# A tenth place in two pieces for expert weights, and another order of gathers and scatters in the loop over experts

## The chip, the cores and the metric

One NeuronCore of a Trainium2 chip. The metric is the device time of one execution in microseconds, lower is better. Engines are named as in the profile: PE is TensorE, DVE VectorE, ACT ScalarE, POOL GpSimd, SP SyncE, whose queue issues nearly all DMAs.

## What is computed

Two transformer blocks on one sequence of 256 tokens of width 1024, all in 32-bit floats. The change lies in the mixture of experts that ends the first block: 32 experts, each token goes to its best ones, gates are a softmax over their logits.

```python
logits = (xt @ router_w + router_b).astype(jnp.float32)
top_vals, top_idx = lax.top_k(logits, TOP_K)
gates = jax.nn.softmax(top_vals, axis=-1)
...
    hcat = xblk @ w_up[e] + b_up[e]
    x_glu = jnp.minimum(hcat[:, 0::2], SWIGLU_LIMIT)
    x_lin = jnp.clip(hcat[:, 1::2], -SWIGLU_LIMIT, SWIGLU_LIMIT)
    act = x_glu * jax.nn.sigmoid(SWIGLU_ALPHA * x_glu) * (x_lin + 1.0)
    return act @ w_down[e] + b_down[e]
...
contrib = y_slots[dest] * gate_sorted[:, None]
out = jax.ops.segment_sum(contrib, tok_sorted, num_segments=N)
```

The second block multiplies two of its results by gate rows that come from a conditioning vector (`x + g1 * ...`, `x + g2 * ...`); the change moves the making of these rows too.

## The kernel before

The program is a row of blocks: `first_mix` (projections and two kinds of attention), `branches` (the rest of the first mix, layer norm, the router's logits and choice), `experts`, `second_mix` and `output`. Between blocks all engines meet.

**Weights of the experts.** An expert has 12 MB of weights: W_up in four chunks and W_down in two, 2048 KB each, rows of 16 KB for each of 128 partitions. Two experts are a pair of 12 chunks; 16 pairs make 192 chunks, numbered 0 to 191. In a pair come the four up chunks of the first expert, the four of the second, then two and two down chunks. Chunk i lies in place i mod 9 (`PLACES`): six places are pairs of slots of `ring`, place 5 (`EXTRA`) is the later two thirds of the buffer `x_xT_xn` (`k.wide`), places 7 and 8 are `more`. `load_expert` issues one DMA for a chunk. SP issues chunks 0 to 8 in `branches`, as their places come free there, and in `experts` `refill` issues chunk i when PE has counted chunk i - 9 as read (`used`, two counts for a chunk). The loop over pairs is unrolled three times (`LOOPED`), so that the places come round.

**A pair on PE** (`pair`). Only the tokens of an expert are worked on: a selection matrix (`keep_tri`) gathers them by matmul (`gather`, in two halves of four tiles, each copied to `xg` by ACT in `gathered`), and another (`selT`) scatters the results back. PE does: up chunks of the first expert (`up_weights`), waits for ACT's copy `hrow`, turns it (`units_turned`), scatters the results of the pair before into four banks (`scatter`), which DVE adds to `acc` (`added`, `collect`), up chunks of the second expert, waits for `hrow`, turns, down chunks of the first expert (`down_weights`), turns the gated selection, gathers both halves for the next pair, and does the down chunks of the second. In the last pair (`tail`) the second half-gather stands between its last two down chunks. Then come the closing products of `acc` with the identity (L1398) and the last scatter.

```python
up_weights(r, turn, at, n, 0)
units_turned(n, 0)
scatter()
up_weights(r, turn, at, n, 1)
units_turned(n, 1)
down_weights(r, turn, at, n, 0)
```

**Around it.** In `branches` DVE makes the gates (L1177 to L1180) and then the choice (L1184, `choose`) that the first gather waits for. ACT writes two diagonal matrices (L1045) from which PE, by products with ones (L965 there, L2154 in `output`), makes the gate rows `gB`; these lie in the first third of `x_xT_xn`. Short products of no use (`fill`) keep PE going in waits.

Of the kernel before, what the change touches and what calls it, by code (L numbers as in the profile page):

```python
# [14 lines left out]
F32 = mybir.dt.float32  # L15
# [3 lines left out]
ALU = mybir.AluOpType  # L19
# [37 lines left out]
UP_CHUNKS = 4  # L57

# [844 lines left out]
def branches(nc, k, a):  # L903
# [9 lines left out]
    gate_ready, gT_done = sem("gate_ready"), sem("gate_turned")  # L913
    gd, ang_ready = sem("gate_diag"), sem("angles")
    gb_done = k.gb_done
# [5 lines left out]
    with k.ctx_block("branches") as blk:  # L921
        @blk.sync
        def _(sp):
# [16 lines left out]
            for i in (MORE, MORE + 1):  # L940
                load_expert(k, sp, a, 0, i)

        @blk.tensor
        def _(pe):
# [18 lines left out]

            def gate_row(half):
                return nc.tensor.matmul(k.ps[:, half, :], k.ones[:, :], k.diag[0][:, half * 512:(half + 1) * 512],  # L965
                                        start=True, stop=True)
# [39 lines left out]
            pe.wait_ge(gd, 1)  # L1006
            logits(0, range(4)).then_inc(log_done, 1)
            gate_row(0)
# [4 lines left out]
            gate_row(1).then_inc(gb_done, 1)  # L1013
# [9 lines left out]
            pe.wait_ge(gate_ready, 1)  # L1023
            for t in range(TT):
                last = nc.tensor.transpose(k.ps[0:E, 6, t * P:(t + 1) * P], k.gate[:, t, :], k.ident[:, :])
            last.then_inc(gT_done, 1)
# [4 lines left out]
        def _(act):  # L1031
# [11 lines left out]
            for n, row in enumerate((GATE1, GATE2)):  # L1043
                for m in range(KD):
                    ins = nc.scalar.activation(k.diag[n][:, m * P:(m + 1) * P], k.ident[:, :], ACT.Copy,  # L1045
                                               scale=k.mod[:, row + m:row + m + 1])
            ins.then_inc(gd, 1)
# [14 lines left out]
            act.wait_ge(gb_done, 1)  # L1062
            act_copy(nc, k.gB[:, 0, :], k.flat[:, 0:1024])
            act.wait_ge(gT_done, 1)
            act.wait_ge(k.selT_zeroed, 1)
            act_copy(nc, k.selT[0:E, :], k.ps[0:E, 6, 0:T]).then_inc(k.selT_ready, 1)
# [35 lines left out]
        def _(dve):  # L1102
# [75 lines left out]
            link(nc.vector.tensor_reduce(k.small[:, 2:4], ex[:, :, :], AX.X, ALU.add))  # L1178
            link(nc.vector.reciprocal(k.small[:, 4:6], k.small[:, 2:4]))
            nc.vector.tensor_tensor(k.gate[:, :, :], ex[:, :, :], bc(k.small[:, 4:6], 2, E), ALU.mult).then_inc(gate_ready, 1)  # L1180

# [5 lines left out]
            nc.vector.tensor_scalar(k.place[:, :, E:E + 2], k.place[:, :, 0:2], float(-CAP), None, ALU.add)  # L1187

# [5 lines left out]

def expert_chunk(k, i):

    i %= PLACES
    if i == EXTRA:
# [4 lines left out]
    return k.ring[:, at:at + 2, :].rearrange("p s n -> p (s n)")  # L1203

# [6 lines left out]
def expert_arrived(k, pe, r, turn, i):  # L1211

    place = i % PLACES
    pe.wait_ge(k.expert_in[place], r * (16 * uses(place)) + turn * (16 * LOOPED * PAIR // PLACES) + 16 * (i // PLACES + 1))
    return expert_chunk(k, i)
# [13 lines left out]
def load_expert(k, sp, a, first, i):  # L1229
# [9 lines left out]
    sp.dma_start(expert_chunk(k, i), src).then_inc(k.expert_in[i % PLACES], 16)  # L1239


def experts(nc, k, a):
# [9 lines left out]
    hot_ready, g_done = k.hot_ready, k.g_done  # L1252
# [8 lines left out]
    scat = (up, rows)  # L1261
# [8 lines left out]
    with k.ctx_block("experts") as blk:  # L1270
# [37 lines left out]
        def _(pe):  # L1308
            def scatter(added=()):
                for t, out in enumerate(scat):  # L1310
# [5 lines left out]
            gather(nc, k, 5, range(4, KD)).then_inc(g_done, 1)  # L1316
            extra = extra_rounds(pe)

            def up_weights(r, turn, at, n, h):
                for q in range(KD):  # L1320
                    if h == 0 and q % 4 == 0:
# [3 lines left out]
                    w = chunk[:, (q % 2) * 2048:(q % 2 + 1) * 2048]  # L1325
# [16 lines left out]
            def down_weights(r, turn, at, n, h, halves=(0, 1)):  # L1342
# [3 lines left out]
                for j in (2 * v + w for v in halves for w in range(2)):  # L1346
                    if j % 2 == 0:
                        chunk = expert_arrived(k, pe, r, turn, at * PAIR + 2 * UP_CHUNKS + 2 * h + j // 2)
                    w = chunk[:, (j % 2) * 2048:(j % 2 + 1) * 2048]
# [1295 lines left out]
```

## Time and profile before

| | |
|---|---|
| median of three runs | 1529.42 us (1527.02 to 1530.88) |
| the profiled execution | 1528.25 us, span of its instructions 1526.5 us |
| busy, share of the span | PE 94%, DVE 38%, ACT 29%, POOL 3% |
| moved by DMA | 516.47 MB, mean 338 GB/s |
| mean granted TensorE clock | 0.998 |
| `experts`, by its first and last products on PE | about 264 to 1182 us |

All rows come from one profiled execution, with times from the start of its span. In a timeline a row is: start, duration, engine, line and operation, output and inputs, count, and in brackets how long the engine had stood idle and what ended that. Rows that follow each other on PE overlap a little, so lengths are better taken from one start to the next. Products of 32-bit floats are recorded as two instructions each (x16 for eight). In a table of stretches each row has the stretch, its length, the busy time of each engine, the granted clock (1.00 is 2.4 GHz), the busy share of the DMA engines and GB/s.

### The profile page before, as it was taken

Reading aid. Unit: us, or ns where it says so; the run is one execution under the profiler, and the core shown is the slowest. Engines: PE = TensorE matmul, PEld = TensorE weight load, DVE = VectorE, ACT = ScalarE, POOL = GpSimd, SP = SyncE. Lnnn points to the kernel's source line nnn. Section 1 sums busy time; section 2 is a strip of 40 time slices with the busy share of each in tenths; the row PEclk is TensorE's granted clock in tenths of the full one; section 3 lists DMA queues with packets and bytes.
Section 4 is the critical chain, followed back from the end, with each engine's and each line's share of the span. In section 5 each row is a group of like instructions: output and inputs, shape, how many; then the busy total and the mean of one; then the engine's idle time right before and its main releaser. Section 6 shows DMA issues by size and latency. Waiting matters only on the chain. (4 is left out here: it accounts for less than half of the span.)

```text
span 1526.5 us, 19835 instructions
## 1 busy us (share of the span) xinstructions
PE 1429.0 (94%) x8005; PEld 846.0 (55%) x8005; DVE 584.2 (38%) x978; ACT 449.3 (29%) x597; POOL 38.4 (3%) x80
## 2 busy tenths in 40 slices
PE   9999999999999999988988989889889999999998
PEld 9987898344334434323423433333333788888887
DVE  4985457211210211210210210210211685777765
ACT  5654543121111112111111111111111536553343
POOL 2000030000000000000000000000000022000000
PEclk9999999999999999999999999999999999999999
DMA  8597999899999999999999999999999461345552
GB/s 284 175 295 258 327 336 411 369 427 428 427 429 427 429 428 427 430 428 428 429 428 428 429 428 428 429 428 429 428 427 367 132 193 56 108 143 191 193 188 88
DMA packets 126918, 516.47 MB, mean 338 GB/s; under 512 B 6885, under 2 KB 95310, under 8 KB 102254
## 3 DMA queue, kind: packets, MB, share of 16 engines
q1 hardware_dynamic: 125998, 513.59, 84.6%
q10 hardware_dynamic: 864, 2.10, 0.4%
q8 instruction: 40, 0.66, 0.2%
q14 instruction: 16, 0.13, 0.0%
HBM read 514.62 MB, written 1.05 MB: 338 GB/s over the span
## 5 line engine op out<-in xcount | busy, mean ns | idle before, releaser
L1329 PE MATMUL ps<-ring,xg 128*64 128x512 f32 x1456 | 324.8, 595 | 25.7 <-DMA ring<-in_expert_w_up 22.7
L1478 DVE TENSOR_TENSOR glu<-ps,bupT 128x512 f32<-128x512 f32 x32 | 22.1, 692 | 720.0 <-PE ps L1338 720.0
L1329 PEld LDWEIGHTS ps<-ring,xg 128*64 128x64 f32 x1456 | 102.4, 137 | 242.5 <-issue 191.5
L88 ACT ACTIVATE hrow<-ps 128x1024 f32<-128x1024 f32 x32 | 32.8, 1024 | 473.4 <-PE ps L1329 473.4
L1354 PE MATMUL ps<-ring,act 128*64 128x512 f32 x608 | 136.3, 596 | 0.0
L2221 PE MATMUL ps<-h_halves,w_hi 128*128 128x512 f32 x352 | 124.2, 399 | 0.1
L2332 DVE TENSOR_TENSOR w_lo<-ring,w_hi 128x2048 fp32r<-128x2048 f32 x36 | 82.5, 2292 | 55.8 <-ACT w_hi L88 55.8
L1329 PE MATMUL ps<-more,xg 128*64 128x512 f32 x416 | 93.0, 595 | 8.7 <-DMA more<-in_expert_w_up 7.5
L2226 PE MATMUL ps<-h_halves,w_lo 128*128 128x256 f32 x348 | 97.7, 281 | 0.0
L88 ACT ACTIVATE w_hi<-ring 128x2048 fp32r<-128x2048 f32 (+1 forms) x38 | 70.8, 1865 | 70.8 <-PE ps L2226 34.6
L88 ACT ACTIVATE y<-ps 64x512 f32<-64x512 f32 x64 | 37.9, 592 | 182.0 <-PE ps L1354 181.6
L1354 PEld LDWEIGHTS ps<-ring,act 128*64 128x64 f32 x608 | 41.2, 137 | 80.3 <-issue 71.4
L88 ACT ACTIVATE in_hi<-ring 128x1024 fp32r<-128x1024 f32 (+1 forms) x72 | 72.2, 1042 | 40.1 <-DMA ring<-in_w_in 16.8
L272 DVE TENSOR_TENSOR in_lo<-ring,in_hi 128x1024 fp32r<-128x1024 f32 x56 | 66.1, 1221 | 41.7 <-ACT in_hi L88 41.7
L541 PE MATMUL ps<-x_hi,in_hi 128*128 128x256 f32 x272 | 78.7, 289 | 0.0
L541 PE MATMUL ps<-x_lo,in_hi 128*128 128x256 f32 x272 | 76.9, 283 | 0.0
L541 PE MATMUL ps<-x_hi,in_lo 128*128 128x256 f32 x272 | 76.8, 282 | 0.0
L2221 PEld LDWEIGHTS ps<-h_halves,w_hi 128*128 128x128 f32 x352 | 66.1, 188 | 16.8 <-DVE h_halves L2389 0.5
L1338 PE MATMUL ps<-ident,hrow 128*128 128x128 f32 x256 | 36.2, 284 | 38.9 <-ACT hrow L88 38.9
L1329 PEld LDWEIGHTS ps<-more,xg 128*64 128x64 f32 x416 | 29.5, 137 | 70.6 <-issue 58.0
L892 PE MATMUL ps<-keep_tri,h 128*128 128x128 f32 x544 | 67.5, 282 | 0.5 <-PEq L921 0.3
L1338 PEld LDWEIGHTS ps<-ident,hrow 128*128 128x128 f32 x256 | 31.0, 194 | 66.2 <-issue 66.2
(419 smaller groups left out, 2256.4 us busy)
## 6 DMA issues: line engine op xcount, KB each, us to landing
ring<-in_expert_w_up SPq DMA_DIRECT2D x91, 2048.0 KB, 36.8
ring<-in_expert_w_down SPq DMA_DIRECT2D x38, 2048.0 KB, 39.3
more<-in_expert_w_up SPq DMA_DIRECT2D x26, 2048.0 KB, 35.4
more<-in_expert_w_down SPq DMA_DIRECT2D x16, 2048.0 KB, 38.8
ring<-in_w_in SPq DMA_DIRECT2D x28, 1024.0 KB, 8.3
ring<-in_w_ada SPq DMA_DIRECT2D x24, 1024.0 KB, 5.8
x_xT_xn<-in_expert_w_up SPq DMA_DIRECT2D x11, 2048.0 KB, 36.8
ring<-in_w_gu SPq DMA_DIRECT2D x22, 1024.0 KB, 5.1
```

Of the source, the lines that this page charges most:

```text
L88: return nc.scalar.activation(out, x, ACT.Copy)
L272: nc.vector.tensor_tensor(k.wlo1[:, n % 4, :], w[:, half * 1024:(half + 1) * 1024], k.whi1[:, n % 4, :].bitcast(F32), ALU.subtract).then_i ...
L541: last = nc.tensor.matmul(out, left, right, start=(j == 0 and kq == 0 and m == 0), stop=(j == 1 and kq == KD - 1 and m == 2), skip_group_c ...
L892: last = nc.tensor.matmul(out, k.h[:, t, (q // 2) * 256 + q % 2:(q // 2 + 1) * 256:2], k.sel[:, t, :], start=(t == 0), stop=(t == TT - 1))
L1329: last = nc.tensor.matmul(up[a2 * CAP:(a2 + 1) * CAP, u, :], k.xg[:, q, h * CAP:(h + 1) * CAP], w[:, c:c + 512], start=(q == 0), stop=(q = ...
L1338: last = nc.tensor.transpose(turned[:, par, j * P:(j + 1) * P], k.hrow[:, hidden_columns(j, par)], k.ident[:, :])
L1354: last = nc.tensor.matmul(down[a2 * CAP:(a2 + 1) * CAP, :], k.act[:, h, m % 4, m // 4, :], w[:, c:c + 512], start=(m == 0), stop=(m == KF ...
L1478: link(nc.vector.tensor_tensor(k.glu[:, :, :, :], g, b[:, 0].to_broadcast(wide), ALU.add))
L2221: last = nc.tensor.matmul(out, w[0][:, q, s], k.hh[:, q, :, :].rearrange("p v t -> p (v t)"), start=(i == 0 and (c, half) != (0, 0)), stop ...
L2226: last = nc.tensor.matmul(out[:, 0:T], w[1][:, q, s], k.hhi[:, q, :], start=False, stop=(i == KD - 1), skip_group_check=True)
L2332: nc.vector.tensor_tensor(k.wlo[i % 2][:, :], k.ring[:, LATE[i % len(LATE)], :], k.whi[i % 2][:, :].bitcast(F32), ALU.subtract).then_inc(w ...
```

## The change

- `PLACES` is 10. Place 9 (`SPLIT`) has two pieces: the first third of `x_xT_xn`, and a buffer `tenth` of 8 KB in each partition. A chunk for it is loaded by two DMAs of half its size, with rows of 8 KB, and is awaited by 32 counts instead of 16. Chunk 9 is issued in `branches` behind chunks 7 and 8. The loop is unrolled five times. A buffer `sigm` is dropped to make room: the sigmoid goes into `act`.
- In a pair the second half-gather goes behind the second up chunk of the first expert in the next pair; the scatter goes behind the up chunks of the second expert, and the turn of that expert between the two down chunks of the first. The last pair does only one half-gather ahead of its last two chunks.
- In `branches` DVE makes the choice ahead of the gates' values; PE turns the gates at the start of `experts`.
- Since the gate rows' buffer is now a piece of place 9, they are made later: PE makes the second in `second_mix` and the first in `output` (`gate_rows`, eight products of 128 columns each with a broadcast column). The two diagonals are dropped.

```diff
-PLACES = 9
+PLACES = 10
-EXTRA, MORE = 5, 7
+EXTRA, MORE, SPLIT = 5, 7, 9
-LOOPED = 3
+LOOPED = 5
...
-            for i in (MORE, MORE + 1):
+            for i in (MORE, MORE + 1, SPLIT):
                 load_expert(k, sp, a, 0, i)
...
+def gate_rows(nc, k, row, banks):
+
+    for m in range(KD):
+        last = nc.tensor.matmul(k.ps[:, banks[m // 4], (m % 4) * P:(m % 4 + 1) * P],
+                                k.mod[:, row + m:row + m + 1].to_broadcast([P, P]), k.ident[:, :], start=True, stop=True)
+    return last
...
+    if i == SPLIT:
+        return [k.wide[:, 0:TT * D], k.tenth]
...
+    place = i % PLACES
+    if place == SPLIT:
+        for half, dst in enumerate(expert_chunk(k, place)):
+            sp.dma_start(dst, src[:, half * 2048:(half + 1) * 2048]).then_inc(k.expert_in[place], 16)
+    else:
+        sp.dma_start(expert_place(k, place), src).then_inc(k.expert_in[place], 16)
...
             def up_weights(r, turn, at, n, h):
                 for q in range(KD):
+                    if h == 0 and q == 4:
+                        pe.wait_ge(acc_done, n * 2 + 1)
+                        gather(nc, k, 5, range(4, KD)).then_inc(g_done, 1)
...
                 units_turned(n, 0)
+                up_weights(r, turn, at, n, 1)
                 pe.wait_ge(selT_ready, n + 1)
                 pe.wait_ge(y_ready, n * 2 + 1)
                 pe.wait_ge(k.bias_in, 32)
-                scatter()
-                pe.wait_ge(acc_done, n * 2 + 3)
-                up_weights(r, turn, at, n, 1)
                 pe.wait_ge(act_ready, n * 2 + 1)
+                scatter(between)
+                down_weights(r, turn, at, n, 0, (0,))
+                pe.wait_ge(acc_done, n * 2 + 4)
                 units_turned(n, 1)
-                down_weights(r, turn, at, n, 0)
+                down_weights(r, turn, at, n, 0, (1,))
...
-                    down_weights(r, turn, at, n, 1, (0,))
-                    gather(nc, k, 3, range(KD // 2, KD)).then_inc(g_done, 1)
-                    down_weights(r, turn, at, n, 1, (1,))
                 else:
-                    pe.wait_ge(acc_done, n * 2 + 4)
-                    for half in range(2):
-                        gather(nc, k, 5, range(4 * half, 4 * half + 4)).then_inc(g_done, 1)
-                    down_weights(r, turn, at, n, 1)
+                    gather(nc, k, 5, range(KD // 2)).then_inc(g_done, 1)
+                down_weights(r, turn, at, n, 1)
```

What stands on PE from the last products of `branches` to the second turn of the first pair, before. Chunks are the rows of `64x512`, a half-gather is `keep_tri,h`, the turns are `ident,hrow`, the scatter is `y,keep_tri`:

```order
L1025 MATMUL ps<-ident,gate 32x128 x2
L892 MATMUL ps<-keep_tri,h 128x128 x8
...
L892 MATMUL ps<-keep_tri,h 128x128 x8
L1265 TENSOR_LOAD rounds
...
L1329 MATMUL ps<-ring,xg 64x512 x16
L1322 REGISTER_ALU
L1329 MATMUL ps<-ring,xg 64x512 x8
L1214 ISA
L1329 MATMUL ps<-ring,xg 64x512 x8
L1338 MATMUL ps<-ident,hrow 128x128 x8
L1364 REGISTER_ALU
L1312 MATMUL ps<-y,keep_tri 128x512 x4
```

And now:

```order
L893 MATMUL ps<-keep_tri,h 128x128 x8
...
L1328 MATMUL ps<-ident,gate 32x128 x2
L1275 TENSOR_LOAD rounds
...
L1345 MATMUL ps<-ring,xg 64x512 x16
L893 MATMUL ps<-keep_tri,h 128x128 x8
L1338 REGISTER_ALU
L1219 ISA
L1345 MATMUL ps<-ring,xg 64x512 x16
L1354 MATMUL ps<-ident,hrow 128x128 x8
L1345 MATMUL ps<-ring,xg 64x512 x8
```

The second half-gather has moved from ahead of the first chunk to behind the second, the turn of the gates has gone behind the first half-gather, and no scatter stands behind the first turn.

What stands on SP from the last expert loads of `branches` on, before and then now (the first two rows that differ in width are the two pieces of chunk 9):

```order
L1239 DMA more<-in_expert_w_up 128x4096
L1239 DMA more<-in_expert_w_down 128x4096
...
L1274 DMA y<-in_expert_b_down 32x1024
...
L1239 DMA ring<-in_expert_w_down 128x4096
```

```order
L1249 DMA more<-in_expert_w_up 128x4096
L1249 DMA more<-in_expert_w_down 128x4096
L1247 DMA x_xT_xn<-in_expert_w_down 128x2048
L1247 DMA tenth<-in_expert_w_down 128x2048
...
L1284 DMA y<-in_expert_b_down 32x1024
...
L1249 DMA ring<-in_expert_w_down 128x4096
```

One chunk more is issued ahead of the loop; in the loop each load now waits for the chunk ten before it.

The last pair on PE now, from the second expert's up chunks to the closing products:

```order
L1345 MATMUL ps<-more,xg 64x512 x8
L1381 REGISTER_ALU
L1322 MATMUL ps<-y,keep_tri 128x512 x4
L1370 MATMUL ps<-more,act 64x512 x8
L1387 REGISTER_ALU
L1354 MATMUL ps<-ident,hrow 128x128 x8
...
L1370 MATMUL ps<-x_xT_xn,act 64x512 x4
L1370 MATMUL ps<-tenth,act 64x512 x4
L1392 MATMUL ps<-ident,sel_gated 128x128 x2
...
L893 MATMUL ps<-keep_tri,h 128x128 x8
...
L1370 MATMUL ps<-ring,act 64x512 x16
...
L1410 MATMUL ps<-acc,ident 128x512 x2
```

The scatter stands where the wait for `hrow` was, and one half-gather is gone (rows 6 below show the old order in time).

## Rows read from the trace of the kernel before

**Rows 1.** Section 2 of the page: GB/s in 40 equal slices
```profile
GB/s 284 175 295 258 327 336 411 369 427 428 427 429 427 429 428 427 430 428 428 429 428 428 429 428 428 429 428 429 428 427 367 132 193 56 108 143 191 193 188 88
```

**Rows 2.** Table of stretches: the hole, the dent and the loop
```profile
264.00:275.00 11.00, 10.69 (x56) 4.92 (x58) 3.86 (x10) 3.96 (x5) 0.00 (x0) 1.00 0.52 180
268.00:271.00 3.00, 3.00 (x16) 1.04 (x14) 0.51 (x1) 1.71 (x3) 0.00 (x0) 1.00 0.00 0
...
290.00:295.00 5.00, 5.00 (x26) 1.60 (x24) 0.01 (x1) 0.00 (x0) 0.00 (x0) 1.00 1.01 390
500.00:1000.00 500.00, 454.03 (x2180) 180.68 (x2180) 94.74 (x171) 83.67 (x113) 0.00 (x0) 1.00 1.01 428
```

**Rows 3.** Waits of PE in 266:1176: us in total, times, longest
```profile
PE ps L1329 <- DMA ring<-in_expert_w_up: 22.7, 19, 1.3
PE ps L1329 <- DMA more<-in_expert_w_up: 7.5, 6, 1.3
PE ps L1329 <- DMA x_xT_xn<-in_expert_w_up: 4.0, 3, 1.3
```

**Rows 4.** Timeline of SP's queue: issues on both sides of the hole
```profile
251.08 0.43 SPq L1239 DMA_DIRECT2D more<-in_expert_w_down  x1
...
270.26 0.37 SPq L1239 DMA_DIRECT2D ring<-in_expert_w_down  x1
```

**Rows 5.** Timeline of PE: two half-gathers and the first four chunks
```profile
261.48 2.15 PE L892 MATMUL ps<-keep_tri,h 128*128 128x128 f32 x16 [0.20 <-DVE keep_tri L876]
263.96 2.12 PE L892 MATMUL ps<-keep_tri,h 128*128 128x128 f32 x16 [0.33 <-PEq L921]
266.40 13.95 PE L1329 MATMUL ps<-ring,xg 128*64 128x512 f32 x64 [0.31 <-issue]
```

**Rows 6.** Timeline of PE: the last pair from its fourth chunk
```profile
1131.90 3.65 PE L1329 MATMUL ps<-ring,xg 128*64 128x512 f32 x16 [1.15 <-DMA ring<-in_expert_w_up]
...
1137.74 3.60 PE L1312 MATMUL ps<-y,keep_tri 128*128 128x512 f32 x8
1141.59 3.65 PE L1329 MATMUL ps<-ring,xg 128*64 128x512 f32 x16 [0.25 <-DVE acc L1445]
...
1148.50 3.60 PE L1329 MATMUL ps<-ring,xg 128*64 128x512 f32 x16
1151.93 3.60 PE L1329 MATMUL ps<-more,xg 128*64 128x512 f32 x16
1156.75 1.13 PE L1338 MATMUL ps<-ident,hrow 128*128 128x128 f32 x8 [1.22 <-ACT hrow L88]
...
1170.70 2.15 PE L892 MATMUL ps<-keep_tri,h 128*128 128x128 f32 x16
1172.78 3.65 PE L1354 MATMUL ps<-ring,act 128*64 128x512 f32 x16
1176.36 1.98 PE L1398 MATMUL ps<-acc,ident 128*128 128x512 f32 x4
```

**Rows 7.** Table of stretches: loads of 1 MB with 1, 2, 4 KB rows
```profile
180.00:186.00 6.00, 5.46 (x48) 5.16 (x50) 4.55 (x6) 2.34 (x3) 0.00 (x0) 1.00 1.10 348
189.00:198.00 9.00, 9.00 (x79) 9.00 (x78) 4.02 (x6) 3.09 (x4) 0.00 (x0) 1.00 1.05 384
...
1487.00:1488.00 1.00, 1.00 (x6) 0.84 (x5) 1.00 (x1) 0.00 (x0) 0.00 (x0) 1.00 1.04 430
```

**Rows 8.** PE in second_mix and at the start of output; clock in 1302:1305
```profile
1190.92 1.06 PE L1610 MATMUL ps<-ident,x_xT_xn 128*128 128x128 f32 x8 [2.31 <-ACT x_xT_xn L1745]
...
1301.73 3.61 PE L2154 MATMUL ps<-x_xT_xn,ones 128*128 128x512 f32 x4 [1.50 <-PEq L1551]
1305.17 1.02 PE L900 MATMUL ps<-x_xT_xn,ident 128*128 128x512 f32 x2
1306.03 1.91 PE L2148 MATMUL ps<-ident,x_xT_xn 128*128 128x128 f32 x16
...
1302.00:1305.00 3.00, 3.00 (x4) 1.21 (x4) 2.48 (x5) 2.88 (x4) 0.00 (x0) 0.50 0.01 3
```

More of the change, by code:

```diff
@@ L57 @@
 UP_CHUNKS = 4
+TENTH_AT = 7568
 NA = 4
@@ L1022, in _ @@
                 .then_inc(pos_done, 1)
[L1023 to L1026, printed above, removed]
             pe.wait_ge(k.hot_ready, 1)
@@ L1203, in expert_chunk, with landings @@
     return k.ring[:, at:at + 2, :].rearrange("p s n -> p (s n)")
+def landings(place):
+    return 32 if place == SPLIT else 16
 def uses(place):
@@ L1213, in expert_arrived @@
     place = i % PLACES
-    pe.wait_ge(k.expert_in[place], r * (16 * uses(place)) + turn * (16 * LOOPED * PAIR // PLACES) + 16 * (i // PLACES + 1))
+    per = landings(place)
+    pe.wait_ge(k.expert_in[place], r * (per * uses(place)) + turn * (per * LOOPED * PAIR // PLACES) + per * (i // PLACES + 1))
     return expert_chunk(k, i)
@@ L1260, in experts @@
     up, down, turned, rows, seT = k.ps[:, 0:2, :], k.ps[:, 2, :], k.ps[:, 3:5, :], k.ps[:, 5:7, :], k.ps[:, 7, 0:T]
-    scat = (up, rows)
+    between, final = (rows, turned), (up, rows)
     def extra_rounds(eng):
@@ L1308, in _, with scatter @@
         def _(pe):
-            def scatter(added=()):
-                for t, out in enumerate(scat):
+            def scatter(banks, added=()):
+                for t, out in enumerate(banks):
                     for half in range(2):
@@ L1314, in scatter @@
                     last.then_inc(sc_done, 1)
-            gather(nc, k, 5, range(4, KD)).then_inc(g_done, 1)
+            pe.wait_ge(k.gate_ready, 1)
+            for t in range(TT):
+                last = nc.tensor.transpose(turned[0:E, 0, t * P:(t + 1) * P], k.gate[:, t, :], k.ident[:, :])
+            last.then_inc(gT_done, 1)
             extra = extra_rounds(pe)
@@ L1401, in _, with gathered @@
             pe.wait_ge(y_ready, extra * (2 * pairs) + 2 * pairs + 1)
-            scatter((1,))
-            fill(nc, k, 7, k.gB[:, 0, 0:512], 1)
+            scatter(final, (1,))
+            fill(nc, k, 7, k.bupT[:, 0:512], 1)
         @blk.scalar
         def _(act):
-            def gathered(n, src):
-                for half in range(2):
-                    act.wait_ge(g_done, n * 2 + half + 1)
-                    act_copy(nc, k.xg[:, 4 * half:4 * half + 4, :].rearrange("p k n -> p (k n)"), src[:, half, :])\
-                        .then_inc(xg_ready, 1)
-            gathered(0, rows)
+            def gathered(n, half, src):
+                act.wait_ge(g_done, n * 2 + half + 1)
+                act_copy(nc, k.xg[:, 4 * half:4 * half + 4, :].rearrange("p k n -> p (k n)"), src).then_inc(xg_ready, 1)
+            gathered(0, 0, rows[:, 0, :])
+            act.wait_ge(gT_done, 1)
+            act.wait_ge(k.selT_zeroed, 1)
+            act_copy(nc, k.selT[0:E, :], turned[0:E, 0, 0:T]).then_inc(selT_ready, 1)
             extra = extra_rounds(act)
@@ L1423, in pair @@
             def pair(n, tail):
+                gathered(n, 1, rows[:, 1, :])
                 for h in range(2):
@@ L1713, in _ @@
             values(heads - 1)
-            fill(nc, k, 0, k.gB[:, 0, 0:256], 1)
+            fill(nc, k, 0, k.bupT[:, 0:256], 1)
         @blk.scalar
@@ L1784, in _ @@
             high(5)
+            act.wait_ge(k.gb_done, 1)
+            for half in range(2):
+                act_copy(nc, k.gB[:, 1, half * 512:(half + 1) * 512], k.ps[:, 4 + 3 * half, :])
             evacuate(2)
@@ L2151, in turned @@
                             ins.then_inc(done, 1)
-            for half in range(2):
-                last = nc.tensor.matmul(k.ps[:, 6 + half, :], k.ones[:, :], k.diag[1][:, half * 512:(half + 1) * 512],
-                                        start=True, stop=True)
-            last.then_inc(k.gb_done, 1)
-            fill(nc, k, 4, k.gB[:, 0, 0:512], 1)
+            gate_rows(nc, k, GATE1, (6, 7)).then_inc(k.gb_done, 1)
+            fill(nc, k, 4, k.bupT[:, 0:512], 1)
             turned(mixed, mn, mt)
@@ L2489, in program @@
                           for n in ("in_hi", "in_lo"))
+        base = nc.sbuf_base
+        with nc.sbuf_tensor("under", [P, TENTH_AT], F32), nc.sbuf_tensor("tenth", [P, SLOT], F32) as v:
+            k.tenth = v[:, :]
         with ExitStack() as early:
@@ L2565, in program @@
                 first_mix(nc, k, a)
-                k.diag = [k.x[:, n, :] for n in range(2)]
                 branches(nc, k, a)
```

93 lines of the change are left out of this document (41 added, 52 removed).

## The prediction

> **What bounds the kernel now.** I read the page first: its shares (in the table above) make TensorE (PE) look like the bound, with 94%, but in slices 10 to 29 of 40 its line of GB/s stands at 427 to 430 [rows 1]. A busy PE that waits for its data in short pieces looks full in such a page, so I asked for single stretches. In 500:1000 the DMA share is 1.01 at 428 GB/s, while PE is busy 454 of 500 us [rows 2]: the expert loop is paced by the transfer of weights. One chunk of 2048 KB (2.097 MB) takes 2.097/428 = 4.90 us, and 12 chunks, one pair of experts, 58.8 us. The list of waits says the same from the other side: in the loop PE waited 28 times for an expert chunk, 34.2 us in all, 1.3 us at the longest [rows 3]. Then I looked for the places where this stream of 192 chunks stands still, because in a stage that is paced by a stream only such holes, and what follows its last chunk, can be won.
>
> There is one hole. In 264:275 only 180 GB/s x 11 us = 1.98 MB were moved, which at 428 takes 4.63 us; so 6.37 us were lost, with 0 GB/s in 268:271 [rows 2]. The queue shows why: the ninth chunk was issued at 251.08, and the next expert chunk only at 270.26, when the first chunk had been read and its place was free [rows 4]. PE begins to read that chunk at 266.40, behind two halves of a gather of about 2.1 us each [rows 5]. A second, small dent follows: 290:295 moved 390 instead of 428, 0.44 us lost [rows 2].
>
> The end of the loop must be read with the beginning. The last wait for a chunk ends at 1131.90, at the fourth chunk of the last pair (index 183) [rows 6]. Chunk 187 then arrives by my count at 1131.90 + 4 x 4.90 = 1151.50; PE starts it at 1151.93, without a wait [rows 6]: 0.43 us behind the stream. From there PE is on its own until the closing products at 1176.36, 24.43 us later [rows 6]. So the last pair is almost in balance: DMA sets its front, PE its back, and an earlier stream is worth something only if PE does not fall behind.
>
> **The change, part by part.**
> *The tenth place.* Chunk 9 (and 19, ... 189, 19 in all) now goes to a place of its own, issued right behind chunk 8 at about 252. Its 4.90 us fill the hole: transfers before the change run out at about 266, now at about 270.7. For the hole to close, chunk 0 must have been read about 1 us before that (issue at 270.26, and 0 GB/s up to 271, [rows 2, 4]). PE gets there sooner: the second half-gather (2.1 us) leaves its way [rows 5], against about 0.5 us for the two turns of the gates that come in, so reading starts near 265 and, at 3.4 us for a chunk, ends near 268.4. I therefore count the whole 6.37 us. Behind it I followed the places one by one with 3.4 us per chunk, a gather (2.1 us) and the ScalarE copy between chunks 1 and 2, and the turn between chunks 3 and 4: the tightest is chunk 4, read by about 287.3, its successor due to start at 270.7 + 4 x 4.90 = 290.3. With 1 us from issue to bytes 2 us remain, so the dent of 0.44 us goes too. Gain of arrival: 6.81 us.
>
> *Its two pieces.* The split chunks move rows of 8 KB where all others move 16 KB. No row shows 8 KB. The nearest on either side: 4 KB rows (the 1 MB loads of w_down) reach 430 GB/s in a full microsecond, no price at all; 1 KB rows (w_in, w_ada) run at 348 and 2 KB rows at 384 in full stretches [rows 7]. From 348 against 428, one 1 KB packet costs an engine 47.1 instead of 38.3 ns, 8.8 ns per packet. A split chunk has 128 packets more, 8 per engine: 0.07 us. With 18 split chunks up to chunk 187 this is 1.27 us. Ends: 0 from the 4 KB row (I exclude a gain, since the bytes are the same), and 18 x (2.097/384 - 4.90 = 0.56) = 10.1 us from the 2 KB row. I take 1.27, near the 4 KB row, which is only half the size away. Arrival of chunk 187: 6.81 - 1.27 = 5.54 us earlier. The extra issue on SyncE takes 0.3 to 0.4 us [rows 4] of a queue that sleeps between uses: nothing.
>
> *The order in a pair.* All of a pair's PE work beside chunks is shorter now (the scatter covers the wait for hrow of the second expert, the gather stays two halves), 12 chunks being 58.8 us of DMA: it costs nothing, DMA covers it, while it lasts. In the last pair it counts. Between chunk 187 and the closing products the wait for hrow goes (4.82 us from chunk to turn, [rows 6], against 3.43 for a chunk alone: 1.39 us), and the second half-gather of the last pair goes (1170.70 to 1172.78: 2.08); the scatter of 3.60 comes in (1137.74 to 1141.34) [rows 6]. Net 0.13 us longer. As chunk 187 is now taken at once on arrival, the 0.43 us of lag is gained. If DMA gave no cover at all, these moves would be worth the same tenth of a microsecond: nothing hangs on them but the room for the 5.54 us to pass. At the end of the loop: 5.54 + 0.43 - 0.13 = 5.84 us earlier. DVE's two additions now stand ahead of the second expert's work, and only the turn of that expert waits for them, a whole chunk (3.4 us) behind the scatter: hidden; without that chunk between, the turn would wait for them, and its products with it.
>
> *Choice ahead of gate values, gate rows made late.* The choice is about half a microsecond earlier; it only brings chunk 0 forward, counted above. The 16 small ScalarE operations that are removed stood in a stretch where the stream of weights set the pace: nothing. The eight products for the second gate replace a fill of two products in second_mix, ahead of a wait of 2.31 us for ScalarE [rows 8], and are of much the same length: nothing, and a few tenths at most if that wait were gone. The eight for the first gate open the output stage. There two products of 512 columns took 3.44 us (1301.73 to 1305.17) with a clock of 0.50, the lower of its two levels, 1.2 GHz, after PE had stood idle 1.50 us, and the turns followed at 1306.03 [rows 8]. Eight products over 128 columns take 2.1 us at full clock, as a half-gather does [rows 5], so 3.4 to 4.2 us there: from 0.1 us of gain (were the clock full, the normalised rows would be waited for instead) to 0.7 us of loss. I take a loss of 0.3 us.
>
> **The sum.** 5.84 - 0.3 = 5.5 us. The profiled execution took 1528.25 us (span 1526.5), so it would take 1522.7; the median of the three runs is 1.2 us above it, and against it the forecast is 1529.4 - 5.5 = 1523.9 us. The runs shown spread over 3.9 us; 0.3% (4.6 us) is about what a measurement of this kernel can tell from no change, and my gain lies just over it.
>
> **The rivals.**
> *The hole only moves.* The stream still pauses, at chunk 10 or a few places later, because PE now does a gather and waits for a ScalarE copy in front of chunk 2. For it: the margins are 2 us, and they rest on my start of 265. If that start is 2 us late, about 2 us of the gain go; if a place is late as well, 4. Or PE loses another stretch at half clock in the last pair or behind it (a stretch of 3.4 us costs 1.7). Against it: the waits in the loop, up to 1.3 us, left the clock at 1.00 [rows 2, 3]. Gain 1.5 to 4.5, about 1526.5 us: within 0.3%.
> *Two pieces cost more than they bring.* Only a split load's price decides: break-even stands at (5.5 + 1.27)/18 = 0.38 us per split chunk. At the rate of the 2 KB row the 19 cost 0.56 us each, 10.6 us: 1523.9 - 1.3 + 10.6 = 1533.2. At the rate of the 1 KB row (348: 1.13 us each, 21.5 us) 1544.1. For it: the rate falls with the row's size, and all these loads are DMAs of 1 MB, as the halves are. Against it: the 4 KB row at 430. The Trainium skill (DMA: Bandwidth & Descriptors, Bandwidth) gives a 1 MB DMA 341 GB/s and asks for at least 1 MiB for 75% of peak; as a price for every half-chunk that would speak against this change. By that rule, as an estimate, a split chunk would take 1.25 us more than a whole one and the kernel would come out near 1546. The trace does not bear it out as a rule on the size of the DMA alone: 1 MB loads of longer rows reach 384 and 430 [rows 7].
>
> **How the numbers follow.** The forecast has 0.60, the moved hole 0.31, the dear pieces 0.09. The range: at the low end a free split (1.3), no loss at the output (0.4) and a favourable measurement (1.3) give 1520.9; at the high end it takes in nearly all of the moved hole, up to 1528.5, and leaves out the dear pieces. Faster by over 0.3%: 0.60; within: 0.31; slower: 0.09.
>
> **What would show it.** Right: GB/s at 425 or more from 264 to 295, chunk 10 issued before 270; arrival of chunk 183 near 1126.5 instead of 1131.90; closing products near 1170.5 instead of 1176.36; waits for chunks also at 184 to 187; output stage 5 to 6 us earlier. Wrong: 0 GB/s anywhere near 270; a mean of the loop under 426 GB/s (dear pieces); a clock under 1.00 in the loop; or the gain present at 1170 and missing at the end.

## The result, and the profile after

| | before | changed |
|---|---|---|
| median (lowest to highest of 5 runs) | 1528.27 us (1525.4 to 1530.88) | 1535.96 us (1533.79 to 1538.61) |
| ratio, with its 95% interval | | 1.0049 (1.0032 to 1.0065) |
| the profiled execution, span | 1528.25, 1526.5 us | 1533.79, 1532.0 us |
| mean granted clock | 0.998 | 0.994 |

The changed kernel is slower by 7.7 us; I had forecast 5.5 us faster. This result lies outside the range, on the side to which I gave 0.09.

The table of stretches of the kernel after (stretch, length, busy time of each engine, granted clock, DMA share, GB/s), to be held against [rows 2]:

```profile
255.00:260.00 5.00, 4.15 (x24) 3.74 (x24) 3.27 (x12) 2.37 (x4) 0.00 (x0) 0.74 0.99 416
260.00:265.00 5.00, 4.17 (x18) 4.04 (x19) 2.80 (x19) 0.32 (x1) 0.00 (x0) 0.50 1.02 429
264.00:275.00 11.00, 9.64 (x46) 5.00 (x47) 3.50 (x7) 3.79 (x5) 0.00 (x0) 0.83 0.83 313
268.00:271.00 3.00, 2.14 (x10) 0.80 (x12) 2.63 (x4) 2.57 (x4) 0.00 (x0) 1.00 1.01 412
275.00:290.00 15.00, 12.98 (x72) 5.94 (x70) 1.54 (x3) 3.29 (x4) 0.00 (x0) 1.00 0.97 391
500.00:1000.00 500.00, 457.06 (x2164) 178.37 (x2162) 96.58 (x171) 85.33 (x113) 0.00 (x0) 1.00 1.01 427
```

268:271, which had 0 GB/s, now has 412: the tenth place does take a chunk there. But the hole is not closed. 264:275 moved 313, not 428, GB/s and 275:290 moved 391, so a pause came a little later. And the column of the granted clock speaks: it is 0.50 in 260:265, the lower of TensorE's two levels (1.2 GHz). The timeline of PE shows what that did:

```profile
255.17 0.66 PE L948 MATMUL ps<-ident,h 128*128 128x128 f32 x4 [0.76 <-DVE h L1127]
...
257.24 2.55 PE L959 MATMUL ps<-rw,fbuf_sgq 128*128 128x32 f32 x12
260.83 0.63 PE L1008 MATMUL ps<-chosen,strict 128*128 128x32 f32 x2 [1.03 <-DVE chosen L1135]
...
263.16 3.78 PE L893 MATMUL ps<-keep_tri,h 128*128 128x128 f32 x16
...
268.86 7.09 PE L1345 MATMUL ps<-ring,xg 128*64 128x512 f32 x32 [1.04 <-issue]
```

PE stands idle 0.76 and 1.03 us, and from 257.24 on its products run at half speed until after the half-gather before the first chunk, which takes 3.78 us instead of 2.15 [rows 5]. For comparison the same stretch of the kernel before, where a product of the first gate's rows stood in both places:

```profile
253.67 1.10 PE L965 MATMUL ps<-x_xT_xn,ones 128*128 128x512 f32 x2
...
256.67 1.72 PE L960 MATMUL ps<-rw,fbuf_sgq 128*128 128x32 f32 x12
258.22 1.10 PE L965 MATMUL ps<-x_xT_xn,ones 128*128 128x512 f32 x2
259.42 0.41 PE L1016 MATMUL ps<-chosen,strict 128*128 128x32 f32 x2
```

So the two gate-row products, which the change moved away, had also kept PE busy while it would have waited for VectorE. The first read of a chunk is at 268.86, not near 265, and SyncE can refill the first place only at:

```profile
272.73 3.74 SPq L1249 DMA_DIRECT2D ring<-in_expert_w_down  x2
```

against 270.26 before [rows 4] and "before 270" in the forecast. In the loop and at its end the timeline of PE shows more:

```profile
542.32 7.09 PE L1345 MATMUL ps<-ring,xg 128*64 128x512 f32 x32 [2.49 <-issue]
...
828.34 7.09 PE L1345 MATMUL ps<-ring,xg 128*64 128x512 f32 x32 [2.27 <-issue]
...
1156.52 3.65 PE L1345 MATMUL ps<-more,xg 128*64 128x512 f32 x16 [1.26 <-DMA more<-in_expert_w_up]
...
1181.71 1.98 PE L1410 MATMUL ps<-acc,ident 128*128 128x512 f32 x4
```

At 542 and 828 PE jumps back to the start of its loop, which is now five pairs long and runs three times; both times it stands 2.3 to 2.5 us for nothing that the profile names. The kernel before has no wait above 1.45 us in its loop. And chunk 187 arrives not at 1146 but at 1156.52; the closing products come 5.35 us after those of before [rows 6], where I had them 5.84 us ahead. In the DMA section of the page the line of the queue for instructions grew, first before, then after:

```profile
q8 instruction: 40, 0.66, 0.2%
```
```profile
q8 instruction: 68, 1.11, 0.3%
```

These are fetches of code, 16 KB a packet. By the packets' own records the kernel before makes none between 415 and 1131 us: its loop of three pairs, once fetched, is run from where it lies. The changed kernel makes 29 in that stretch, one about every 25 us, 12 in a turn of its loop.

**How runs are compared below.** The stage ahead of the experts starts up to 4 us earlier or later from one execution to the next. So from each profile I take two distances from one mark, the first router product, which is, before and after:

```profile
251.89 1.94 PE L960 MATMUL ps<-rw,fbuf_sgq 128*128 128x32 f32 x16 [0.34 <-ACT fbuf_sgq L88]
```
```profile
252.47 1.94 PE L959 MATMUL ps<-rw,fbuf_sgq 128*128 128x32 f32 x16 [0.34 <-ACT fbuf_sgq L89]
```

A is the distance to the start of the products on the last up chunk (187), B that to the closing products. Before: B = 1176.36 - 251.89 = 924.47. After: A = 904.05, B = 929.24. So 4.8 of the 5.5 us between the two profiled spans lie between the mark and the closing products. The profiled execution of the changed kernel was the fastest of its five, 2.2 us below their median, and that of the unrolled kernel below was the slowest of its six, 2.6 us above; the distances are therefore compared with each other, and the medians with each other.

| run | median, us | ratio to before (95%) | A | B | code packets |
|---|---|---|---|---|---|
| changed | 1535.96 | 1.0049 (1.0032 to 1.0065) | 904.05 | 929.24 | 68 |
| fillers back | 1530.63 | 1.0013 (1.0005 to 1.0022) | 901.21 | 926.30 | 68 |
| fillers, loop unrolled | 1531.54 | 1.0018 (1.0009 to 1.0028) | 900.68 | 926.95 | 64 |
| nine places, new order | 1528.30 | 0.9994 (0.9985 to 1.0003) | 899.20 | 924.84 | 40 |
| the same again | 1528.79 | 1.0002 (0.9993 to 1.0011) | 899.28 | 924.25 | 40 |
| before, unrolled | 1533.37 | 1.0030 (1.0019 to 1.0042) | | 930.25 | 64 |
| before, one place split | 1529.57 | 1.0004 (0.9995 to 1.0013) | | 925.96 | 40 |
| tenth place used once | 1526.83 | 0.9990 (0.9981 to 0.9999) | 897.00 | 922.10 | 46 |
| the same again | 1526.82 | 0.9991 (0.9982 to 1.0000) | 897.04 | 923.57 | 46 |
| used once, no fillers | 1531.26 | 1.0013 (1.0004 to 1.0022) | 900.22 | 925.51 | 46 |
| used three times | 1527.12 | 0.9990 (0.9981 to 0.9999) | 895.51 | 921.87 | 46 |

A repeats to 0.1 us where a kernel was profiled twice, B to 1.5 us, medians to 0.5 us. Code packets are those of the whole execution. The kernel before has another order in its last pair, so A is not given for it.

### The profile page after: what moved, and what is told of

The parts are those of the page before. It is cut to its first block and busy times, and to the rows that moved or that the text cites. A ratio compares the mean times of both kernels' runs of the same rounds, so it can differ in the third digit from the quotient of the medians.

```text
span 1532.0 us, 19871 instructions
## 1 busy us (share of the span) xinstructions
PE 1440.0 (94%) x8009; PEld 847.8 (55%) x8009; DVE 587.0 (38%) x978; ACT 443.9 (29%) x581; POOL 38.7 (3%) x80
## 5 line engine op out<-in xcount | busy, mean ns | idle before, releaser
L1345 PE MATMUL ps<-ring,xg 128*64 128x512 f32 x1248 | 280.4, 596 | 33.8 <-DMA ring<-in_expert_w_up 18.3
L1345 PEld LDWEIGHTS ps<-ring,xg 128*64 128x64 f32 x1248 | 86.0, 137 | 206.7 <-issue 162.4
L1459 DVE TENSOR_TENSOR acc<-acc,ps 128x1024 f32<-128x1024 f32 x33 | 40.3, 1222 | 223.7 <-PE ps L1322 223.7
L1345 PE MATMUL ps<-x_xT_xn,xg 128*64 128x512 f32 x304 | 69.9, 595 | 8.7 <-DMA tenth<-in_expert_w_up 4.8
L893 PEld LDWEIGHTS ps<-keep_tri,h 128*128 128x128 f32 x528 | 66.3, 200 | 13.3 <-issue 13.2
L893 PE MATMUL ps<-keep_tri,h 128*128 128x128 f32 x528 | 71.1, 289 | 0.0
```

What stands on the lines that cost most here:

```text
L893: last = nc.tensor.matmul(out, k.h[:, t, (q // 2) * 256 + q % 2:(q // 2 + 1) * 256:2], k.sel[:, t, :], start=(t == 0), stop=(t == TT - 1))
L1345: last = nc.tensor.matmul(up[a2 * CAP:(a2 + 1) * CAP, u, :], k.xg[:, q, h * CAP:(h + 1) * CAP], w[:, c:c + 512], start=(q == 0), stop=(q = ...
L1459: nc.vector.tensor_tensor(k.acc[:, t, :], k.acc[:, t, :], flat(banks[t]), ALU.add).then_inc(acc_done, 1)
```

## The experiments

My theory after the result: three things ate the gain. The clock (without its two filler products PE waits, runs at half clock, and reads chunk 0 late), the code (a loop of five pairs is fetched anew in every turn), and the split. The rivals: the new order of a pair is itself dearer, the tenth place brings nothing (the hole only moves), or the split is the whole loss.

**The fillers back.** Two products that nobody reads, in the places where the gate rows had been:

```diff
             logits(0, range(4)).then_inc(log_done, 1)
+            fill(nc, k, 0, k.bupT[:, 0:512], 1)
             turn(1, 0)
             logits(1, (0,))
             turn(1, 1)
             logits(1, (1, 2, 3)).then_inc(log_done, 1)
+            fill(nc, k, 1, k.bupT[:, 0:512], 1)
```

> The changed kernel, with two products of no use (512 columns each) put back on PE where the gate rows' products stood in the choice. In the changed kernel's profile the clock is at 0.50 from 257.5 to 267 and PE reads the first chunk from 268.86, so chunk 10 is issued at 272.7, after the tenth chunk has landed. Theory clock: the missing products let PE idle long enough for the clock to fall; with them back the clock stays at 1.00, reading starts near 264.5, the hole behind chunk 9 closes and the time falls by 2 to 4 us, to 1532 to 1534. Theory code (the loop over five pairs is fetched anew each turn, and these fetches slow the stream of weights): the rest of the loss, about 5 us against the kernel before, stays. If the clock falls all the same, the time stays at 1536.

1530.63 us, 5.3 below the changed kernel and more than the 2 to 4 that I expected. Its table of stretches and the timeline of PE:

```profile
264.00:275.00 11.00, 9.46 (x52) 4.29 (x51) 3.41 (x7) 3.67 (x5) 0.00 (x0) 1.00 1.01 392
275.00:290.00 15.00, 12.98 (x69) 5.69 (x69) 3.04 (x6) 3.54 (x4) 0.00 (x0) 1.00 1.01 419
```
```profile
255.74 1.10 PE L901 MATMUL ps<-bupT,ident 128*128 128x512 f32 x2
...
260.28 1.10 PE L901 MATMUL ps<-bupT,ident 128*128 128x512 f32 x2
...
263.19 2.15 PE L893 MATMUL ps<-keep_tri,h 128*128 128x128 f32 x16 [0.40 <-DVE keep_tri L877]
...
267.25 7.09 PE L1347 MATMUL ps<-ring,xg 128*64 128x512 f32 x32 [1.21 <-issue]
```

From the mark to the first read it is now 13.29 us (267.25 - 253.96) instead of 16.39, and the clock is 1.00. That is the start that I had forecast: 265 lies 13.1 us behind the mark of the kernel before. Adding 2.2 us of useless work took 5.3 us off the median, of which the profiled pair shows 2.9 in B. So the clock is shown as a cause. But the kernel is still behind before, with its hole nearly closed, so something else costs about as much as the place brings.

**Nine places in the new order.** All of the change that is not the tenth place, its split or the longer loop, with the fillers:

```diff
-PLACES = 10
+PLACES = 9
...
-EXTRA, MORE, SPLIT = 5, 7, 9
+EXTRA, MORE, SPLIT = 5, 7, 99
...
-LOOPED = 5
+LOOPED = 3
...
-            for i in (MORE, MORE + 1, SPLIT):
+            for i in (MORE, MORE + 1):
```

> The changed kernel with nine places and a loop over three pairs as before, no split chunk, and the two products of no use put back; the order in a pair, the choice and the late gate rows stay as changed. Theory code and theory split both expect no fetches of code between 430 and 1140, a chunk every 4.894 us, and the time of the kernel before, 1528 to 1529. Theory order (the gather between chunks and the late scatter cost something of their own) expects 1531 or more.

1528.30, no different from before. The order and the late gate rows are neutral, as forecast, and this is the base for what follows.

**The kernel before with its loop unrolled**, all 15 pairs as straight code. `LOOPED` sets PE's loop and the one in which SP issues the loads, so both are unrolled:

```diff
-LOOPED = 3
+LOOPED = 15
```

> The kernel before with LOOPED = 15: the same instructions in the same order, nine places, no split chunk, but the code of 15 pairs stands in a row, so that it must be fetched all through the loop. Theory code expects a chunk every 4.94 instead of 4.894 us once PE waits for chunks, 0.046 x 178 = 8 us in all, so 1534 to 1537. Theory split (the two pieces are what slows the stream) expects no change, 1528.

1533.37, 4.6 us slower and just under the 1534 to 1537 that I expected, without a split, a tenth place or a new order. 64 code packets instead of 40. The timeline of PE, at one of three long waits for a chunk (the others are at 607 and 1080), and at the last chunk of the first expert of the last pair (index 183):

```profile
843.96 3.65 PE L1329 MATMUL ps<-ring,xg 128*64 128x512 f32 x16 [2.58 <-DMA ring<-in_expert_w_up]
...
1139.08 3.65 PE L1329 MATMUL ps<-ring,xg 128*64 128x512 f32 x16 [1.15 <-DMA ring<-in_expert_w_up]
```

From its mark at 254.02 that is 885.06 us; before it was 1131.90 - 251.89 = 880.01 [rows 6]. So code that does not stay in place costs 5.05 us up to there, though it runs the same products. The rows say that PE waited for DMA: the weights come later.

**The split alone**, in the kernel before: the 21 chunks of place 8 as two DMAs with rows of 8 KB.

```diff
-    sp.dma_start(expert_chunk(k, i), src).then_inc(k.expert_in[i % PLACES], 16)
+    if i % PLACES == 8:
+        for half in range(2):
+            s = slice(half * 2048, (half + 1) * 2048)
+            sp.dma_start(expert_chunk(k, i)[:, s], src[:, s]).then_inc(k.expert_in[8], 16)
+    else:
...
```

> The kernel before with the 21 chunks of place 8 loaded as two DMAs with rows of 8 KB each. Theory split puts the whole slowing (0.46 us per ten chunks) on the one split chunk in ten: 21 x 0.46 = 9.7 us slower, 1538. Theory code expects at most the price of the prediction, 21 x 0.07 = 1.5 us: 1528 to 1530.

1529.57, ratio 1.0004 with 1 inside its interval. Chunk 183 is read at 1133.57 - 252.20 = 881.37 from the mark, 1.36 us later than before, for 20 split chunks: 0.07 us each, as I had estimated. It is read from one profile of each kernel, so it is luck that it fits to the digit; by the packets of the stream the 18 split chunks between 18 and 187 cost 1.5 us, 0.08 us each. The rule of the Trainium skill that I had weighed (DMA: Bandwidth & Descriptors, Bandwidth) is not borne out as a price on the size of a DMA: my estimate from it was 1.25 us for each split chunk.

**Fillers back and the loop unrolled**, against the first run: the stalls at the two back-edges go, the fetches stay.

```diff
-LOOPED = 5
+LOOPED = 15
```

> The changed kernel with the two filler products back, and LOOPED = 15, so the matmul loop of five pairs becomes 15 pairs in straight code. Everything else is the run with the filler products (1530.63 us, ratio 1.0013). It separates the two prices of long code: the two stalls at the loop's back-edges (2.36 and 2.35 us before the first product of pairs 6 and 11) are gone, the instruction fetches (68 packets there) stay. Theory A, stalls at back-edges reach the end only as far as the stream of chunks has no lead over TensorE: they are part of the loss, at most 2 x 2.4 = 4.7 us: 1526 to 1529, ratio 0.998 to 1.0005. Theory B, the fetches alone make the loss by slowing the weight stream (late loop 4.94 us per chunk against 4.89) and by small stalls of their own, and the back-edges are absorbed: 1530.6, ratio 1.001 to 1.002. Theory C, straight code is fetched no better, only later: within 1 us above, 1531 to 1532.

1531.54 us, not below the looped version (1530.63). The waits of 2.4 us at the back-edges are gone, and A is only 0.5 us less. PE was ahead of its data there, so these stalls, the most visible rows of the new profile, cost next to nothing. Theory A is out. The time lies in the range of theory C, the ratio in that of B; this run does not tell them apart, and both leave the cost with the fetches.

**The tenth place used once.** If the place is worth something and long code costs, then the loop must stay at three pairs. With ten places a whole number of turns needs five (60 chunks), with nine it needs three (36). So chunk 9 goes to the tenth place and all later ones to the nine others; the first pair is written out, three follow the loop of 4 x 3:

```diff
...
+def place_of(i):
+
+    return i if i <= SPLIT else (i - 1) % PLACES
...
+                pair(r, 0, 0, r * PAIRS, False)
                 with pe.Fori(0, TURNS) as g:
-                    for at in range(LOOPED):
+                    for at in range(1, 1 + LOOPED):
                         pair(r, g, at, r * PAIRS + g * LOOPED + at, False)
-                pair(r, TURNS, 0, r * PAIRS + (PAIRS - 1), True)
+                for at in (1, 2, 3):
+                    pair(r, TURNS, at, r * PAIRS + TURNS * LOOPED + at, at == 3)
...
```

> The changed kernel with the filler products back, and the tenth place used once only: chunk 9 lands there in its two pieces while the place of chunk 0 is not free yet, and every later chunk goes through the nine places (chunk i at place (i-1) mod 9). The first pair is written out, the loop is three pairs long again and runs four times, the last three pairs are written out. The order of products is that of the changed kernel. Theory A (the prediction's gain is real, and was eaten by the clock, by code of five pairs and by the split): against the same order with nine places (1528.30 us, ratio 0.9994) the hole in the stream closes and nothing is paid but one split chunk, so the closing products come 4 to 5.5 us earlier: 1523.0 to 1524.5, ratio 0.9960 to 0.9972; fetch packets 40 to 50, late loop 4.89 to 4.90 us per chunk. Theory B (the hole only moves, the rival of the prediction): the stream stands again before the next place is free, and of the lead less than 2 us is left at chunk 187: 1526.5 to 1528.5, ratio 0.998 to 1.000. Theory C (written-out pairs cost as the long loop did): 1528 to 1531.

1526.83: faster than before by 2.0 us, but not by the 4 to 5.5 that my theory wanted. The result lies between theories A and B, and the table of stretches says why:

```profile
264.00:275.00 11.00, 9.64 (x50) 4.45 (x52) 2.71 (x4) 3.61 (x5) 0.00 (x0) 1.00 1.01 393
...
310.00:345.00 35.00, 33.10 (x171) 13.86 (x172) 4.76 (x11) 7.95 (x11) 0.00 (x0) 1.00 0.97 405
```

The stream is full where the hole was and pauses where the tenth place is given up: chunks 18 and 19 took 5.93 and 5.85 us instead of 4.90, since chunk 19 waits for chunk 10 where it would have waited for chunk 9. By the packets of the stream, added up chunk by chunk, chunks 7 to 17 took 50.1 us, against 55.3 with nine places: of these 5.2 us of lead 2.0 are given back there. A is 2.2 us less than with nine places. This stage has 14 code packets instead of 8, from the pairs that are written out; at the 0.2 us a packet found below, an estimate of 1.2 us, that is about what is left.

**The same without the fillers**, which shows the clock's part without the loop of five pairs:

```diff
-            fill(nc, k, 0, k.bupT[:, 0:512], 1)
-            fill(nc, k, 1, k.bupT[:, 0:512], 1)
```

> As the run with the tenth place used once, but without the two filler products: what the half clock in the choice costs when nothing else is changed for the worse. Theory A (the half clock delays the first read of chunk 0 and so the first refill, and the hole in the stream is kept; the difference between the changed kernel and its version with the fillers was 5.3 us): 4 to 5.5 us above the run with the tenth place once, 1527.5 to 1529.5, ratio 0.999 to 1.0010, granted clock 0.5 in 260 to 265 us. Theory B (part of the 5.3 us came from the combination with the long loop): 1 to 3 us above it. Theory C (the fillers matter only for where the loop's fetches fall): no difference.

```profile
260.00:265.00 5.00, 3.97 (x18) 3.70 (x18) 2.82 (x19) 0.51 (x2) 0.00 (x0) 0.50 0.99 419
```

1531.26: 4.4 us slower, A 3.2 us later. Theory A. Without the fillers the tenth place is worth less than nothing.

**Three uses, and both neighbours again.** The tenth place takes chunks 9, 19 and 29, with three pairs ahead of the loop and one behind, so as much code; the two neighbours are unchanged:

```diff
-    return i if i <= SPLIT else (i - 1) % PLACES
+    return i % (PLACES + 1) if i < 3 * (PLACES + 1) else (i - 3) % PLACES
...
```

> As the run with the tenth place used once, but the tenth place takes chunks 9, 19 and 29, and the change to nine places comes at chunk 39 instead of chunk 19: three pairs are written out ahead of the loop of three, one behind it, so there is as much code as there. With the place used once, the stream led the kernel before by 6.0 us at chunk 16 and by 4.1 us at chunk 24: chunks 18 and 19 took 5.93 and 5.85 us instead of 4.90, since from there each must wait for one chunk more. Theory A (part of the hole moves to where the tenth place is given up, and is smaller the later that is, because TensorE needs less time for a pair than its chunks take to arrive): chunks 18 and 19 take 4.90 us, the lead stays 5.5 to 6.0 us to the end, 1 to 2 us below the run with the place once: 1524.5 to 1526, ratio 0.9975 to 0.9985. Theory B (the whole 2 us come back at chunks 38 and 39): the lead is 4 us behind them and the time that of the place used once, 1526.5 to 1527.5.

> The kernel with the tenth place used once, again, on the same chip as its two neighbours in this group, since its runs lay 7 us apart (1524.29 to 1531.52). Theory A: 1526.8 or below, ratio 0.9980 to 0.9992, and 1.5 to 4 us below the nine places in the new order (the lead of the stream at chunk 187 was 3.1 us greater). Theory B (the lead at chunk 187 does not reach the end): within 0.7 us of the nine places.

> Nine places in the new order with the filler products, again, as the base for the two others of this group: no tenth place, no split, loop of three pairs. As before: 1528.3, ratio 0.9985 to 1.0003, under both theories.

The stretch and two waits of the run with three uses:

```profile
310.00:345.00 35.00, 33.10 (x167) 13.23 (x167) 4.76 (x11) 6.98 (x9) 0.00 (x0) 1.00 1.01 426
```
```profile
1146.24 3.65 PE L1360 MATMUL ps<-ring,xg 128*64 128x512 f32 x16 [1.24 <-DMA ring<-in_expert_w_up]
...
1169.01 3.65 PE L1385 MATMUL ps<-more,act 128*64 128x512 f32 x16 [1.16 <-DMA more<-in_expert_w_down]
```

The pause in 310:345 is gone (426 GB/s) and nothing like it came at chunk 39, so A falls by another 1.5 us: as to where the lead goes, theory A held. The median did not follow: 1527.12 against 1526.82 beside it. The second row shows where some of it stays: PE now waits 1.16 us more for the last chunk of all. One of the two profiles with a single use has the same wait (1.35 us), the other has none. Why that chunk is sometimes late I did not find out. The base repeated at 1528.79, so the place used once is worth 1.5 to 2.0 us against it; its ratio to before, 0.9990 and 0.9991, is below 1 in both groups, the second by the edge of its interval. These are the only versions that beat both kernels, by less than the 0.3% that I had set.

## Why the prediction was wrong

- **Bound and hole: right, with the size too large.** The loop is paced by the stream of weights, and the hole in 264:275 is there and can be filled: in the runs with the tenth place and fillers chunks 7 to 17 took 50.1 to 50.9 us, in those with nine places 55.2 to 56.1. That is 5.2 us, where I counted 6.81: 264:275 moves 384 to 393 GB/s in these runs, never the 425 that I named as a sign. In the changed kernel the same chunks took 53.6 us, so it fills less than half of the hole.
- **"Reading starts near 265": the first step that failed.** I counted what leaves PE's way (a half-gather) and not what its removal uncovers. The two gate-row products were costed nowhere in the part on the choice; of their removal there I counted only the 16 ScalarE operations that feed them, as nothing. They were PE's cover for two waits for VectorE. Without them: idle 0.76 and 1.03 us, clock 0.50, start at 268.86; with useless products in their place, the start that I forecast. The price is 4.4 us by medians (3.2 in A) in the clean pair of runs, and 5.3 (2.8 in A) in the changed kernel. My own rival, "The hole only moves", named a start 2 us late as its condition and half clock as a danger, but put the danger in the last pair.
- **LOOPED 3 to 5: the second step, which was missing.** The prediction has no term for it; I read it as bookkeeping, since 60 chunks fit ten places. It is a length of code. Unrolling alone cost 4.6 us by medians and 5.05 at chunk 183 in the kernel before. The Trainium skill (Runtime: NRT & Kernel Launch, Instruction fetch mechanics) says that TensorE holds 2048 instructions, fetched by DMA in blocks of 16 KiB, and that a jump to a block outside what it holds forces a fetch first. The trace agrees: no code packets between 415 and 1131 us in the three-pair loop, 2.3 to 2.5 us at each back-edge of the five-pair loop. The same section calls the cost of crossing a block "mostly hidden" and unrolling the better choice; here the unrolled loop was slower than the one that fits, and the measurement decides.
- **The split: right.** 1.27 us forecast for 18 chunks, 1.36 measured for 20. The rival that made it decide (0.09) is right in the sign only by luck: slower, but by none of its mechanism.
- **The order and last pair: right.** Nothing, by two runs with nine places (924.84 and 924.25 against 924.47 in B).
- **The gate rows at the output: a loss of 0.3 us forecast, none measured.** The change moves this stage by at most 0.3 us either way; whether the clock falls ahead of it moves it by 0.4 to 0.8. In both kernels PE stands idle 1.50 us there. The changed kernel, and behind it the kernel with the tenth place used once, in its second profile:

```profile
1307.29 2.02 PE L1181 MATMUL ps<-ident,mod 128*128 128x128 f32 x16 [1.50 <-PEq L1557]
...
1310.88 2.23 PE L2159 MATMUL ps<-ident,x_xT_xn 128*128 128x128 f32 x16 [0.71 <-DVE x_xT_xn L2360]
```
```profile
1300.31 3.64 PE L1183 MATMUL ps<-ident,mod 128*128 128x128 f32 x16 [1.50 <-PEq L1575]
```

  The same eight products take 2.02 us in one and 3.64 in the other. At half clock the turns stand 129.71 us behind the closing products, in the kernel before 129.67 (1306.03 - 1176.36 [rows 6, 8]); at full clock 128.93 to 129.24 in the new order, and 128.97 and 129.22 in the two runs of the old kernel, unrolled and with a split. And from the closing products to the end it is 350.3 us in the changed kernel and 350.1 in the one before.
- **What is left without both faults** is 1.5 to 2.0 us by medians, not 5.5. With three uses A is 3.7 us ahead of nine places, B 2.4 to 3.0, the median 1.7. From the last up chunk to the closing products I counted 24.56 us (24.43 + 0.13); it is 25.0 to 26.5 in these runs, up to 1.35 us of it waiting for the last chunk of all.

The sum by measured terms, for B: -5.2 for the hole, +1.3 for 18 or 19 pieces, +5.05 for the code, +2.9 for the clock: +4.05 us, against 4.77 measured. Each term comes from one pair of profiles and B repeats to 1.5 us only (in the unrolled kernel B itself is 5.78 longer, not 5.05), so the fit is no closer than that. The medians differ by 7.7 us and the two profiled executions by 5.5: the profile of the changed kernel shows its fastest execution. Where its slower ones lose 2.2 us more no profile shows, and it stays open.

Not tried: a loop of five pairs with fewer instructions in a pair, and one filler alone.

## What to carry to other kernels

Before you move a product off a path, look at what it covers: if the engine would wait there, the product is filler for the clock, and useless work left in its place can pay (2.2 us of it bought 4 to 5). A buffer count sets the length of a software loop through the least common multiple with the chunks of a turn, and a loop's code has a size of its own: look for the instruction queue's packets inside the loop, and where they appear, keep the extra buffer for the pairs written out ahead of it. The most striking new wait need not be the cost: here the back-edge stalls were absorbed and the quiet fetches were not.

## What the runs showed of the hardware

**Code fetches beside a full stream of weights** went with a delay of more than their bytes. The unrolled kernel has 24 more packets than before, 0.39 MB or 0.9 us at 428 GB/s, but lost 5.05 us up to chunk 183, about 0.2 us a packet. Counted by all bytes moved, the stream of chunks 18 to 187 was only 2.2 us slower (834.96 against 832.78 us); the rest is that a chunk completes later than the mean of the stream: chunk 187 by 4.2 to 4.7 us in the kernels that fetch all through the loop, by 1.4 to 2.3 in the others.

The landings of a chunk's 16 parts, which its semaphore counts, show more. In the kernel before, the first and the last part of a chunk land 2.4 to 2.5 us apart all through chunks 40 to 189. In the unrolled kernel this distance grows from 2.0 us (mean of chunks 20 to 29) to 7.9 (180 to 189). In the first profile of the tenth place used once it stays at 2.0 to 2.2 us while the loop of three pairs runs (chunks 40 to 159), and grows to 3.6 in the pairs that are written out behind it. So it grows where code is fetched, and it is half of the parts that fall behind: of chunk 187 in the unrolled kernel eight land 896.7 to 899.0 us behind the mark, the other eight 901.4 to 904.6. A chunk is there only with its last part. The records do not name the DMA engines, and how a fetch holds these parts back stays open.

**The clock** fell sooner than I thought it could. In the changed kernel PE had been idle 0.34, 0.76 and 0.47 us ahead of the slow products at 257.24 (2.55 us against 1.72), of which the kernel before has the first and the last too; the granted clock was 0.74 in 255:260 and 0.50 in 260:265. It fell before the second gap that a filler covers (1.03 us, ahead of 260.83). With a product of 1.1 us in place of each of the two it stayed at 1.00; the first filler alone was not tried. In the expert loop the waits of up to 1.3 us left the clock at 1.00, but longer ones did so only at times: with the fillers back it fell behind both back-edge stalls (2.36 and 2.35 us; clock 0.72 in 540:546 and in 827:833), in the changed kernel behind neither (2.49 and 2.27), in the unrolled kernel behind one of three waits of 2.6 us (0.66 in 607:612). And with the same 1.50 us of idle time ahead of the output it fell in 2 of the 12 profiles.
